# One hybrid decoder step on one Trainium2 core: a gated recurrence's decay factors as running products, in chunks of 64 tokens

## The reference, cut to what matters

```python
logf = log(lb + (1 - lb) * sigmoid(fa));  key = (1 - lb) * sigmoid(-fa);  q = silu(qa)
cum = cumsum(logf)                                   # within a chunk
o_inter = (q * exp(cum)) @ S                         # S: state before the chunk
scores[t, s] = sum_k q[t, k] * key[s, k] * exp(cum[t, k] - cum[s, k])   for s <= t
o_intra = scores @ v
S_new = exp(cum_last) * S + (key * exp(cum_last - cum)).T @ v
o = rms_norm(o, norm_g) * silu(ga)
```

## Time and profile before

| | |
|---|---|
| median of 3 runs | 777.7 us (775.05 to 783.83) |
| the profiled execution | 776.89 us, of which the span of its instructions is 775.2 us |
| mean granted clock of PE | 0.977 of full speed |
| PE busy | 731.6 us (94% of the span) |
| DVE busy | 490.9 us (63%) |
| ACT busy | 264.8 us (34%) |
| POOL busy | 237.6 us (31%) |
| HBM traffic | 147 GB/s over the span |

### The profile page before, as it was taken

How to read it: one execution, slowest core, us unless ns; L and a number is a source line. 1 busy time by engine, 2 the same in 40 slices (tenths; PEclk the granted TensorE clock), 3 DMA queues, 4 the chain that set the end, 5 groups by cost and what they waited for, 6 DMA issues and landing times. The chain is left out here.

```text
span 775.2 us, 13387 instructions
## 1 busy us (share of the span) xinstructions
PE 731.6 (94%) x4554; PEld 432.1 (56%) x4554; DVE 490.9 (63%) x923; ACT 264.8 (34%) x571; POOL 237.6 (31%) x344
## 2 busy tenths in 40 slices
PE   4989999999999999999999999999998997989994
PEld 3544444544444555677655567774477775764441
DVE  0222399999999755455555645555489986394535
ACT  3114710225675222222223222225546444430000
POOL 1550014036998232222222222221143471450000
PEclk9988999999999999999999999999999996899998
DMA  9930063060400687988888898861050000420611
GB/s 237 294 100 1 2 216 116 0 224 0 170 0 1 203 265 246 346 278 287 277 253 261 252 320 299 278 193 44 7 211 1 2 1 0 147 85 3 202 53 41
DMA packets 61092, 114.68 MB, mean 148 GB/s; under 512 B 8258, under 2 KB 21523, under 8 KB 61027
## 3 DMA queue, kind: packets, MB, share of 16 engines
q1 hardware_dynamic: 30034, 50.96, 20.8%
q0 software_dynamic: 12512, 40.34, 15.7%
q10 hardware_dynamic: 18480, 22.55, 8.8%
HBM read 106.60 MB, written 7.23 MB: 147 GB/s over the span
## 5 line engine op out<-in xcount | busy, mean ns | idle before, releaser
L473 PE MATMUL banks<-wbuf,xT 128*128 128x512 f32 (+1 forms) x448 | 144.9, 520 | 0.0
L339 POOL DMA_DIRECT2D arena<-in_cache_v x128 | 68.7, 537 | 199.9 <-issue 199.9
L473 PEld LDWEIGHTS banks<-wbuf,xT 128*128 128x128 f32 (+1 forms) x448 | 64.7, 171 | 74.1 <-issue 68.7
L733 PE MATMUL banks<-wbuf,xT 128*128 128x512 f32 (+1 forms) x288 | 99.5, 524 | 0.0
L1242 DVE TENSOR_REDUCE small<-banks 128x1 f32<-128x512 f32 x32 | 22.1, 690 | 92.9 <-PE banks L664 92.9
L1223 DVE MAX8 small<-arena 64x8 f32<-64x2112 f32 x32 | 75.1, 2348 | 1.4
L1225 DVE MATCH_REPLACE8 arena<-small,arena 64x2112 f32<-64x2112 f32 x32 | 74.7, 2334 | 0.0
L647 PEld LDWEIGHTS banks<-ident,arena 128*128 128x128 f32 x512 | 56.4, 140 | 21.5 <-issue 20.7
L647 PE MATMUL banks<-ident,arena 128*128 128x128 f32 x512 | 68.1, 276 | 0.1
L719 PE MATMUL banks<-xT,arena 128*128 128x288 f32 x256 | 67.4, 406 | 0.0
L1030 ACT COPY wbuf<-banks 128x512 f32<-128x512 f32 x64 | 37.2, 581 | 70.0 <-PE banks L647 70.0
(11 more groups left out here) (258 smaller groups left out, 1143.2 us busy)
## 6 DMA issues: line engine op xcount, KB each, us to landing
arena<-in_cache_k SPq DMA_DIRECT2D x128, 256.0 KB, 3.4
arena<-in_cache_v POOLq DMA_DIRECT2D x128, 256.0 KB, 3.7
wbuf<-in_w_in ACTq DMA_DIRECT2D x8, 2048.0 KB, 11.8
arena<-in_w_in ACTq DMA_DIRECT2D x8, 512.0 KB, 5.7
wbuf<-in_w_out SPq DMA_DIRECT2D x1, 2048.0 KB, 9.0
xT<-in_w_out SPq DMA_DIRECT2D x1, 2048.0 KB, 13.6
arena<-in_x_prompt SPq DMA_DIRECT2D x4, 512.0 KB, 8.4
out<-wbuf SPq DMA_DIRECT2D x1, 2048.0 KB, 9.6
```

Source lines behind the costliest of these rows:

```text
L339: e.dma_start(buf[n % 2][:, i, :], cache[bass.ds(pg, 1), 0].rearrange("a p h d -> p (a h d)")).then_inc(arrived[n % 2], 16)
L473: mm = pe.matmul(psum[a * NS:a * NS + ROWS[t], n % PB, 0:w // split], xT[:, c, t * P:t * P + ROWS[t]], wbuf[:, WB[g], c, a * w // split:(a ...
L733: mm = pe.matmul(psum[a * NS:a * NS + ROWS[t], bank, 0:512 // split], xT[:, c, t * P:t * P + ROWS[t]], wbuf[:, WB[g], c, a * 512 // split: ...
```

## The change

- Decays are products of the forget gate `fg` instead of exponentials of sums: log, scan, differences and their exponentials go. `first_decay` multiplies all queries by `fg`; at each level `longer_runs` multiplies neighbouring runs' products, and `decay_by` multiplies, tile by tile, the queries of right halves and the keys of left halves in place, all on DVE. After the last level queries and keys carry the factors that the chunk stage needs. POOL and ACT have no part in it.
- Chunks are 64 tokens, levels 7, jobs 32. A job is 8 matmuls 64 x 64, for each head one in each column half of the array; its `copy_predicated` is 256 wide. Jobs are dealt evenly over steps 2 to 29.
- Gate tiles 2, 3 and 4 move into the loop, one of their 8 matmul groups a step (`gate_piece`, steps 0 to 25), all into bank 0. SiLU of `ga` on ACT, and with it POOL's product with `norm_g`, come behind the loop.
- On DVE ahead of the loop: `prompt_bias`, `forget_gate`, `gather_out` of the last sequence, `input_key`, `first_decay`; the masks' copies go to step 0. On ACT SiLU of `qa` goes ahead of the second gate tile's copy.
- The chunk stage runs over 8 chunks, two a tile: both increments of a tile as one group, 8 new states, outputs in two halves of 64 partitions. `turn_normed(0)` and the sample tokens' outputs now wait for the outputs of all tiles (`oc_ev`), since they share PSUM banks.
- Buffers: keys are decayed in place (`kE = ky`), `x` rows, `z`, and the spread queries and values get places of their own; one constant and its load go.

```diff
-LEVELS = [0, 1, 2, 4, 8, 16, 32, 64]
+LEVELS = [0, 1, 2, 4, 8, 16, 32]
+CH = 64
+NC = SEQ // CH
...
-        LEAD, STEP = 2, 3
-        LAST = LEAD + STEP * NLEV
-        def level_of(a):
-            l, c = (a - LEAD) // STEP, (a - LEAD) % STEP
-            return (l, c) if 0 <= l < NLEV else (None, c)
+        LEAD, TAIL = 2, 2
         def jobs_of(a):
+            n = NA - LEAD - TAIL
+            return range(len(JOBS) * (a - LEAD) // n, len(JOBS) * (a - LEAD + 1) // n) if LEAD <= a < NA - TAIL else range(0)
+        UPDATES = {x: n for n, x in enumerate(x for x in JOBS if x[0])}
+        GATES = [(GA_, t) for t in (2, 3, NT)]
+        def gate_piece(a):
+            return (GATES[a // (KC + 1)], a % (KC + 1)) if a < len(GATES) * (KC + 1) and a % (KC + 1) < KC else None
...
                 token_tile(GA_, 1, everything, 1, 0)
-                token_tile(GA_, 2, everything, 2, 0)
-                token_tile(GA_, 3, everything, 0, FILL_NO[GA_, 0] + 1)
...
+                        pe.wait_ge(qe_ok, UPDATES[l - 1, c] + 2 if l > 1 else 1)
+                        if l > 1:
+                            pe.wait_ge(ke_ok, UPDATES[l - 1, c] + 1)
+                    kk, qq = kE, (qa if l == 0 else qE)
                     for h in range(HA):
-                        mm = pe.matmul(psum[0:w, n % 3, h * w:(h + 1) * w], kk[:, h, c0:c0 + w], qq[:, h, c0:c0 + w],
-                                       start=True, stop=True, skip_group_check=True)
+                        for a in range(2 if c < NT else 1):
+                            c0 = c * P + a * CH
+                            mm = pe.matmul(psum[a * CH:(a + 1) * CH, 1 + n % 2, h * CH:(h + 1) * CH], kk[:, h, c0:c0 + CH],
+                                           qq[:, h, c0:c0 + CH], start=True, stop=True, skip_group_check=True)
                     mm.then_inc(lv, 1)
...
                         prompt_logits(a)
-                        if a == 0:
-                            token_tile(GA_, NT, everything, 1, FILL_NO[GA_, 1] + 1)
                         for n in jobs_of(a):
                             level_job(n)
+                        piece = gate_piece(a)
+                        if piece:
+                            token_tile(*piece[0], [piece[1]], FB, FILL_NO[piece[0]] if piece[0][1] > 2 else FILL_NO[GA_, 0] + 1)
...
                 filled((GA_, 0), 0)
-                act.wait_ge(f_ok, HA)
-                nc.scalar.activation(dec, dec, ACT.Ln).then_inc(ln_ok, 1)
+                nc.scalar.activation(qa, qa, ACT.Silu).then_inc(q_ok, 1)
                 filled((GA_, 1), 1)
-                nc.scalar.activation(qa, qa, ACT.Silu).then_inc(q_ok, 1)
                 nc.scalar.activation(gB[:, 0:NT], gB[:, 0:NT], ACT.Silu).then_inc(gb_ok, 1)
                 nc.scalar.activation(gB[0:NS, NT], gB[0:NS, NT], ACT.Silu).then_inc(gb_ok, 1)
-                filled((GA_, 2), 2)
-                filled((GA_, 3), 0)
...
-                    if a == LEAD + 3 * STEP:
-                        nc.scalar.activation(ga[:, 0:NT], ga[:, 0:NT], ACT.Silu).then_inc(gate_ok, 1)
-                        nc.scalar.activation(ga[0:NS, NT], ga[0:NS, NT], ACT.Silu).then_inc(gate_ok, 1)
                     if a < NA:
-                        l, step = level_of(a)
-                        if step == 1 and l is not None and l + 1 < NLEV:
-                            act.wait_ge(diff_ok, l + 1)
-                            act.wait_ge(diff_k_ok, l + 1)
-                            nc.scalar.activation(dec[:, :, 0:span(l + 1)], dec[:, :, 0:span(l + 1)],
-                                                 ACT.Exp).then_inc(dec_ok, 1)
...
-                        if a == LAST + 2:
-                            act.wait_ge(dl_ok, 2)
-                            nc.scalar.activation(dec, dec, ACT.Exp).then_inc(dl_ex, 1)
...
                         prompt_exponential(a)
+                    piece = gate_piece(a - 1) if a else None
+                    if piece and piece[1] == KC - 1:
+                        filled(piece[0])
                     if a >= 1:
                         probs_out(a - 1)
+                nc.scalar.activation(ga[:, 0:NT], ga[:, 0:NT], ACT.Silu).then_inc(gate_ok, 1)
+                nc.scalar.activation(ga[0:NS, NT], ga[0:NS, NT], ACT.Silu).then_inc(gate_ok, 1)
...
+                def first_decay():
+                    dve.wait_ge(f_ok, HA)
+                    dve.wait_ge(q_ok, 1)
+                    nc.vector.tensor_tensor(qE, qa, fg, ALU.mult).then_inc(qe_ok, 1)
+                def longer_runs(l):
+                    left, right = runs_of(l)
                     if l > 1:
+                        dve.wait_ge(run_ok, l - 1)
+                    n = span(l) // (2 * LEVELS[l])
+                    nc.vector.tensor_tensor(decay[2 * LEVELS[l]][:, :, 0:n].unsqueeze(3), left, right, ALU.mult).then_inc(run_ok, 1)
+                def decay_by(l, c):
+                    left, right = chunk_runs(l, c)
+                    keys, queries = chunk(kE, l, c)[0], chunk(qE, l, c)[1]
+                    if l > 1:
+                        dve.wait_ge(run_ok, l - 1)
+                        dve.wait_ge(ke_ok, UPDATES[l - 1, c] + 1)
+                    dve.wait_ge(qe_ok, UPDATES[l - 1, c] + 2 if l > 1 else 1)
+                    nc.vector.tensor_tensor(queries, queries, left.to_broadcast(list(queries.shape)), ALU.mult).then_inc(qe_ok, 1)
+                    nc.vector.tensor_tensor(keys, keys, right.to_broadcast(list(keys.shape)), ALU.mult).then_inc(ke_ok, 1)
...
+                prompt_bias()
                 forget_gate()
-                prompt_bias()
+                gather_out(NSEQ - 1)
                 input_key()
-                masks_in()
-                running_sums()
+                first_decay()
                 for a in range(NA + 2):
                     if a < NA:
-                        l, step = level_of(a)
-                        if step == 0 and l is not None and l + 1 < NLEV:
-                            differences(l + 1)
                         mask_and_max(a)
+                        if a == 0:
+                            masks_in()
                         for n in jobs_of(a):
                             scores_out(n)
...
+                            l, c = JOBS[n]
+                            if l and c == 0:
+                                longer_runs(l)
+                            if l:
+                                decay_by(l, c)
...
+                def chunk_states(t):
+                    pe.wait_ge(turned_ev, t + 1)
+                    if t:
+                        pe.wait_ge(st_ok, HA * 2 * t)
                     for h in range(HA):
+                        for a in range(2):
+                            r = slice(a * CH, (a + 1) * CH)
+                            mm = pe.matmul(psum[:, 4 + a, h * P:(h + 1) * P], kdT[r, t, h * P:(h + 1) * P],
+                                           ia[r, t, h * P:(h + 1) * P], start=True, stop=True, skip_group_check=True)
                     mm.then_inc(kv, 1)
-                    turn_gated(c)
-                    if c >= 2:
-                        pe.wait_ge(oc_ev, c - 1)
+                def chunk_out(t, a):
+                    r = slice(a * CH, (a + 1) * CH)
+                    return r, psum[r, (2, 6)[a] + t % 2, :]
+                def within_chunks(t):
+                    if t >= 2:
+                        pe.wait_ge(oc_ev, t - 1)
                     for h in range(HA):
...
+                        for a in range(2):
+                            r, out = chunk_out(t, a)
+                            mm = pe.matmul(out[:, h * P:(h + 1) * P], sc[r, t, h * CH:(h + 1) * CH],
+                                           ia[r, t, h * P:(h + 1) * P], start=(h == 0), stop=(t == 0 and a == 0),
+                                           skip_group_check=True)
+                def from_before(t):
+                    for a in range(2):
+                        cc = 2 * t + a
+                        if cc == 0:
+                            continue
+                        pe.wait_ge(st_ok, HA * cc)
+                        r, out = chunk_out(t, a)
+                        for h in range(HA):
+                            mm = pe.matmul(out[:, h * P:(h + 1) * P], qE[:, h, cc * CH:(cc + 1) * CH],
+                                           states[(cc - 1) % 2][:, h * P:(h + 1) * P], start=False, stop=True,
+                                           skip_group_check=True)
+                        mm.then_inc(oc, 1)
+                for t in range(NT):
+                    chunk_states(t)
+                    turn_gated(t)
+                    within_chunks(t)
+                    from_before(t)
...
+                    if t == 0:
+                        pe.wait_ge(oc_ev, NT)
...
-                    dve.wait_ge(kv, c + 1)
+                    dve.wait_ge(kv, c // 2 + 1)
                     if c >= 2:
-                        dve.wait_ge(oc, c)
+                        dve.wait_ge(oc, c - 1)
...
```

(13 more changed lines are left out.)

196 lines of the change are left out of this document (59 added, 137 removed).

## The result

Each kernel was run 20 times: 777.62 us before (774.84 to 783.83), 769.33 us after (764.45 to 776.13). The ratio is 0.9881, interval 0.986 to 0.9903: 1.2% faster. The forecast was 772.3, in a range of 759 to 786; of its three classes it gave most to "within 1%", and the result is just outside that.

A forecast was written before the change was run, and what follows sets the result against it. Neither PE nor DVE alone was taken to bound the old loop; PE was to pace the new one. Start, loop, seam, chunk stage and clock: 776.9 - 13.5 - 15.6 + 8.4 + 12.6 + 3.5 = 772.3 us, range 759 to 786.

The forecast's parts named there:

- within 1%: Whole kernel: time less than about 1%, 8 us, from that before; chance 0.46.
- Start of the full steps: Ahead of the loop: step 2 begins at 547.4 instead of 560.86 us; gain 13.5 us, between 12 and 15.
- The loop: Step 2 to last product: PE sets the pace, 90.6 us instead of 106.2; gain 15.6, at best 23, at worst 2.
- The seam: Between loop and chunk stage: other engines wait for SiLU of `ga` and POOL's products; cost 8.4 us, between 7 and 10.
- The chunk stage: Block's start to the first `turn_normed`: 31.6 us instead of 19.05; cost 12.6 us, 7.5 to 19.
- the cycle: Chunk stage, per tile: 6.05 us, since the next increments wait for both new states.
- The pairs: Chunk stage: pairs of 64-row records cost 0.21 us in the increments and 0.16 us in the outputs within chunks.
- The clock in the second block: Chunk stage begins at 1.2 GHz after PE stands at the seam; cost 3.5 us, between 0 and 17.
- Rival 1: Loop's saving not given back: chunk-stage pair loads hidden, no loop turnarounds or waits, clock back early; 759 us, chance 0.31.
- Rival 2: Clock stays low through the whole chunk stage; 787.6 us, slower than before; chance 0.10.
- Rival 3: Loop and chunk stage: column and row halves take turns; 797 us, slower; chance 0.08.
- rival 4: Loop: DVE sets the pace, its updates taking 0.7 us instead of 0.33; 8 us more, 780; chance 0.12.

The follow-up runs named there:

- run 20: Not a label but a count: each kernel was run 20 times, 777.62 us before and 769.33 us after the change.
- e5: Changed kernel with all gate tiles and SiLU of `ga` ahead of the loop, SiLU of `gB` ahead of the second gate copy: 770.24 us, ratio 0.9773.
- e2: Changed kernel with SiLU of `gB` ahead of the second gate tile's copy on ACT: 764.85 us, ratio 0.9824.
- e7: Changed kernel with three state buffers instead of two: one execution, 777.15 us; increments start 4.21 us apart.
- e8: Changed kernel with nearly all decay products left out: one execution, 7.4 us less on DVE, 0.01 us in the loop.
- e1: Changed kernel with SiLU of `ga` back in the loop, behind the last gate piece: 769.67 us, ratio 0.9885.
- e4: Changed kernel with 22 extra matmuls on PE behind the loop's last product: 777.18 us; the chunk stage 28.19 us instead of 29.86.
- e9: Changed kernel with the chunk stage's column halves issued one after the other: one execution, 786.86 us (before there 788.68); cycles 6.15 us instead of 5.15.
- e6: Changed kernel with POOL's last two `values_apart` waiting for the chunk stage's last outputs: one execution, 774.45 us (before on that chip 786.25).
- e3: Changed kernel with the column halves of the loop's level jobs issued one after the other: 776.72 us, ratio 0.9984.
- e12: e11 with level jobs dealt from step 0 instead of step 2: 768.25 us, ratio 0.974 of the two medians.
- e11: Changed kernel with the edits of e5, e6 and e7 together: 769.49 us, ratio 0.9777.

## Why the prediction came out as it did

- **Start of the full steps, -13.5: right** (-13.4). The order on ACT was read correctly, down to the wait for the first exponential. What was missed is the wait's second price, the clock. The two tiles' 13.9 us are also work moved and not saved: e5 puts the tiles back ahead of the loop, and the loop shrinks by their time.
- **The loop, -15.6: mechanism right, sum short of one term.** Measured -12.4. e2 gives 90.9 us for the 90.6 worked out, so the failed step is a term that was put at nothing: the part on the clock prices the seam and the wait ahead of `turn_normed` and looks at the loop's tail, where 2.4 GHz did stay, but not at its start, though the same text had PE waiting there. The fall costs 2.9 us (e2, e7). That 90.9 meets 90.6 so closely is partly luck: PE's work was worked out as 87.6 us and its waits as 3, and in e2 PE is busy for 89.23 and idle for 1.65. Other terms were off but did no harm: a job takes 0.46 to 0.62 us as forecast, an update on DVE 0.42 us and not 0.33, and e8 shows that this doesn't matter.
- **The seam, +8.4: right in kind**, 9.3 measured. No term had POOL's DRAIN, 1.4 us behind its last record; the other 0.5 went the other way, since ACT's last copy ended 2.1 us ahead of DVE's last product and not 1.5. (ACT's three rows add up to 3.8 and not to the 3.7 of the sum.)
- **The chunk stage, +12.6: too high.** Measured +10.8, or +9.1 without the low clock (e1, e4 and e5 all have 28.2 us). The failed term is the cycle: 6.05 forecast, 5.15 measured, three times, and the first tile another 0.9 (e4: the second tile's increments start 6.9 us behind the block's start, not 7.8). The pairs were priced at 0.21 and 0.16 us, from the 64-row logits; they take 0.11 both, the lower bound given for the increments, as long as the halves are issued in turn (e9). The chain itself, second state behind PE's first outputs, was right (e7), and DVE held up by POOL too (e6).
- **The clock in the second block, +3.5: near, on the high side.** 1.7 at its start (e4) and up to 1.1 between the two `turn_normed`, 2.8 together.
- **Rival 1** (saving not given back) was right that the pairs of the chunk stage cost no more than 0.11 us, but the cost did not fall to its 7.5. **Rival 2** (clock low through the chunk stage) didn't come: 5.3 us at 0.50, then full until 675. **Rival 3** is refuted for both stages (e3, e9) and **rival 4** by e8.
- **The class.** The forecast lay 0.6% below the kernel before. The profiled pair, freed of the 1.7 us ahead of the loop, agrees to 0.1 us, but by terms that cancel; the medians are 8.3 apart. One part of the difference may be the clock: the fall at the loop's start lasted 6.8 us in the profiled execution of after, and it lasts 0 to 10.2 in the nine traces with the same wait; the mean clock is 0.977 there, and the 20 runs go from 764 us at 0.985 to 776 at 0.966. How long it lasted in the other 19 wasn't traced, so the rest stays open.

## What to carry to other kernels

A short wait of PE ahead of a dense stretch can cost twice: behind waits of 1.66 us (eight of nine traces), 2.24, 2.54 and 3.48 us the clock stood at 0.50 for 3.4 to 10.2 us. So list each wait that a change leaves or makes, and price the low clock behind it too. Small fp32 matmuls in the two halves of the array should be issued in turn, half by half. Work that is put at the end of a block because nothing needs it there is still waited for by all engines; and before a POOL instruction is moved to a quieter place, look what POOL does next and which DVE instructions stand beside it, since one of them may be held up for the whole run.

## What was not expected of the hardware

- The clock's fall behind the same wait comes in some executions and not in others: the same loop code took 96.0 us without a fall (e7), 99.1 to 99.2 us with one of 6.8 us (after, e4, e6) and 100.8 with one of 10.2 (e9).
- POOL's DRAIN at the block's end lasted 1.40 us beyond its last record; it did so in the kernel before too (655.64 to 657.04), where nothing waited for it. DVE's in the kernel before lasted 0.05 us.
- Records of 128 rows by 64 columns follow each other every 0.058 us in one column half, though each one's load record is 0.138 us long, and a record of the other half starts 0.007 us beside each if it is next in order.
- Four DVE instructions of 1.14 us together stretched to 11.65 us beside six POOL instructions (e12), 9.39 of them for one instruction; beside four POOL instructions in e11 four such took 5.93 us, one of them ending behind each of the last three.
